# Subtracting the low parts of 64 weight tiles on VectorE between the passes of the expert selection, instead of on GpSimd

## The chip, the cores and the metric

The kernel runs on one core of a Trainium2 chip. The metric is the device time of one execution in microseconds (us); lower is better. The engines are named as the profile names them: PE (TensorE), DVE (VectorE), ACT (ScalarE), POOL (GpSimd) and SP (SyncE, which here only issues DMAs).

## The reference: what is computed

One decoder layer for 512 tokens of width 2048: an attention and state-space mixer, a normalisation, and then a layer of very many small experts (PEER). Only the expert layer matters here:

```
s1, s2 = q[..., :half] @ sub_keys1.T, q[..., half:] @ sub_keys2.T      # 128 scores per side and head
v1, i1 = top_k(s1, 16);  v2, i2 = top_k(s2, 16)
cand = v1[..., :, None] + v2[..., None, :]                              # 256 sums per head
top_s, pos = top_k(cand, 16);  ids = cand_id[pos];  g = softmax(top_s)  # 8 heads x 16 experts a token
act = gelu(einsum('td,tkd->tk', h, u_tab[ids]))
out = einsum('tk,tkd->td', g * act, v_tab[ids])
```

There are 16384 experts, each with a row of 2048 numbers in `u_tab` and one in `v_tab`. The kernel does not gather these rows for three of the four blocks of 128 tokens: it multiplies the 384 tokens of these blocks with all experts, and weighs the products with a matrix of gates that is zero where an expert was not picked.

## The kernel before, in words

The products are wanted in nearly full float32 precision. So each operand is cut into a high part (ACT rounds it to fp32r, a format that PE multiplies fast) and a low part (the value less its high part), and each product is three matmuls: high by high, high by low, low by high.

The expert weights come in units of 128 x 1024. For a unit of `u_tab`, SP loads it into one of four buffers (`pre_raw`), ACT writes the high part into one of two places of `split` (line 861), an engine subtracts it from the raw unit and writes the low part beside it, and PE runs 24 matmuls of 128 x 384 (line 1615). Because `split` has two places, ACT may write the high part of unit n only when PE is done with unit n-2, and the low part of n can only follow.

The stage of this case lies between 1277 and 1720 us. It is called the expert selection, and goes over the four blocks of tokens m = 0 to 3. In each block:

- DVE runs `select(m)` (lines 1210 to 1250). It finds the best 16 of 128 scores in 16 rows (8 heads by 2 sides) in four passes: the largest 8 (MAX8, line 1191), their places and their removal (FIND_INDEX8 and MATCH_REPLACE8, lines 1194 and 1195), the next 8 (line 1198), their places (line 1201). Then it forms the 256 sums (line 1221), runs the same four passes over 8 rows of 256, and turns the places into expert numbers (lines 1224 to 1240; the longest steps are lines 1235 to 1237, which run twice). From line 1242 on it needs the exponentials of line 879.
- Beside it PE runs `ahead(m)`: 16 units, that is 16 x 24 matmuls, whose results do not depend on the selection. There are 64 such units "made ahead" in all. In the kernel before, POOL subtracts the low parts (line 643).
- ACT writes the high parts, applies the GELU to finished pairs of units, and only after the last unit of the block computes the exponentials (line 879) that line 1242 on DVE waits for.
- Then PE turns the picks of block m (for m = 0 to 2), and makes the gates of block m-1 (line 1638), while DVE writes the one-hot matrices for them (`one_hots`, lines 1258 and 1261). Only then does PE go on to `ahead(m+1)`.

Each engine takes its instructions in the order in which they are written, and a semaphore wait at the head holds back all that stands behind it. After each dependent step of the selection DVE waits for its own last instruction (`step`). After a block, the gates are stored by SP, and from block 2 on SP issues the loads of the next block's units only behind these stores.

Of the kernel before, what the change touches and what calls it, by code (L numbers as in the profile page):

```python
# [19 lines left out]
TB = S // P  # L20
# [12 lines left out]
PH, PK = 8, 16  # L33
# [10 lines left out]
RAWS = 4  # L44
# [7 lines left out]
WIN_PAIRS = AHEAD * GT // TB // 2  # L52
WIN_UNITS = 4 * WIN_PAIRS

F32 = mybir.dt.float32
# [3 lines left out]
ALU = mybir.AluOpType  # L59
# [51 lines left out]
def over(ap, axis, n):  # L111

    wide = ap.unsqueeze(axis)
    shape = list(wide.shape)
    shape[axis] = n
    return wide.to_broadcast(shape)
# [95 lines left out]
def decoder_layer(nc, x_rows, x_cols, c_cols, pos_cols, w_ada, b_ada_cols, w_slices, conv_w, conv_b,  # L212
                  dt_bias, a_log, d_skip, norm_w, sinks, w_out, ln1_g, ln1_b, w_q, keys, u_units, u_tab, v_tab,
                  ln2_g, ln2_b, out):
    with ExitStack() as ctx:
        def sb(name, shape, dt=F32):
            return ctx.enter_context(nc.sbuf_tensor(name, shape, dt))
# [14 lines left out]
        def place(region, off, *dims):  # L232

            start = taken.get(region, off)
            taken[region] = start + math.prod(dims)
            return at(start, *dims)
# [52 lines left out]
        split = sb("split", [P, 2, 2, UNIT], F32R)  # L289
# [90 lines left out]
        pair_v = place("e", WIN + 4 * K, PH, PK)  # L380
        pair_i = place("e", WIN + 4 * K, PH, PK).bitcast(U32)
# [13 lines left out]
        pre_raw = wt  # L395
# [186 lines left out]
        def _(pool):  # L582
# [53 lines left out]
                        .then_inc(wout_split, 1)  # L636


            for m in range(TB):
                with pool.Fori(0, WIN_PAIRS) as i:  # L640
                    for j in range(4):
                        pool.wait_ge(pre_high, i * 4 + (m * WIN_UNITS + j + 1))
                        nc.gpsimd.tensor_tensor(split[:, j % 2, 1, :], pre_raw[:, j, :], split[:, j % 2, 0, :].bitcast(F32), ALU.subtract)\  # L643
                            .then_inc(pre_split, 1)

            pool.wait_ge(topk_done, TB)
            pool.wait_ge(g_ps, DT // 4 + HOTS * OH // 4)
# [271 lines left out]
        def _(dve):  # L919
# [154 lines left out]
            with dve.Fori(0, TB) as b:  # L1074
                step = Steps(dve, dve_own, b * MIX_STEPS + start)
# [100 lines left out]
            with dve.Fori(0, TB) as m:  # L1176
                step = Steps(dve, dve_own, m * 10 + start1, held)
# [7 lines left out]
                assert step.n == 10, step.n  # L1185
            own.n += TB * 10

            def best16(rows, step):

                for values, _, source, _ in rows:  # L1190
                    ins = nc.vector.max(values[:, 0:8], source)
                step(ins)
                for values, indices, source, scratch in rows:
                    nc.vector.max_index(indices[:, 0:8], values[:, 0:8], source)
                    ins = nc.vector.match_replace(scratch, values[:, 0:8], source, NEG)
                step(ins)
                for values, _, _, scratch in rows:
                    ins = nc.vector.max(values[:, 8:16], scratch)
                step(ins)
                for values, indices, _, scratch in rows:  # L1200
                    ins = nc.vector.max_index(indices[:, 8:16], values[:, 8:16], scratch)
                step(ins)


            dve.wait_ge(h2_high, 1)
# [7 lines left out]
            def select(m):  # L1213
                step = Steps(dve, dve_own, m * TOP_STEPS + start2, held)
                dve.wait_ge(sc_ready, m + 1)
                dve.sem_inc(held, 1)
                best16([(top_v[:, side, h, :], top_i[:, side, h, :], sc[:, side, h, :], rest[:, side, h, :])
                        for side in range(2) for h in range(PH)], step)
                step(nc.vector.tensor_copy(top_f, top_i))

                step(nc.vector.tensor_tensor(cand, over(top_v[:, 0, :, :], 3, PK), over(top_v[:, 1, :, :], 2, PK), ALU.add))
                flat = [cand[:, h, :, :].rearrange("p a b -> p (a b)") for h in range(PH)]
                best16([(pair_v[:, h, :], pair_i[:, h, :], flat[h], flat[h]) for h in range(PH)], step)
                step(nc.vector.tensor_copy(pick_sum, pair_v[:, :, 0]))
                nc.vector.tensor_tensor(pair_v, pair_v, over(pick_sum, 2, PK), ALU.subtract).then_inc(pair_sub, 1)

                nc.vector.tensor_scalar(part_u[:, 0, :, :], pair_i, 4, None, ALU.logical_shift_right)
                step(nc.vector.tensor_scalar(part_u[:, 1, :, :], pair_i, 15, None, ALU.bitwise_and))
                step(nc.vector.tensor_copy(part_f, part_u))
                dve.wait_ge(parts_read, m + 1)  # L1230
                dve.sem_inc(held, 1)
                for side in range(2):
                    flat = hits.rearrange("p a b c -> p (a b) c")
                    places = part_f[:, side, :, :].rearrange("p a b -> p (a b)")
                    step(nc.vector.tensor_tensor(flat, over(iota[:, 0:PK], 1, PICKS), over(places, 2, PK), ALU.is_equal))
                    step(nc.vector.tensor_tensor(hits, hits, over(top_f[:, side, :, :], 2, PK), ALU.mult))
                    step(nc.vector.tensor_reduce(part_id[:, side, :, :].rearrange("p a b -> p (a b)"), flat, AX, ALU.add))
                step(nc.vector.scalar_tensor_tensor(part_f[:, 0, :, :], part_id[:, 0, :, :], float(NKEY), part_id[:, 1, :, :],
                                                    ALU.mult, ALU.add))
                nc.vector.tensor_copy(ids[:, bass.ds(m, 1), :].rearrange("p a (b c) -> p (a b) c", c=PK), part_f[:, 0, :, :])  # L1240
                dve.wait_ge(pair_exp, m + 1)
                step(nc.vector.tensor_reduce(pick_sum, pair_v, AX, ALU.add))
                step(nc.vector.reciprocal(pick_sum, pick_sum))
                nc.vector.tensor_tensor(gates[:, bass.ds(m, 1), :].rearrange("p a (b c) -> p (a b) c", c=PK), pair_v,
                                        over(pick_sum, 2, PK), ALU.mult).then_inc(topk_done, 1)
                dve.wait_ge(topk_done, m + 1)
                dve.sem_inc(sc_used, 1)
                assert step.n == TOP_STEPS, step.n

            def one_hots(m):  # L1250
# [4 lines left out]
                for n in range(P // OH):  # L1255
# [7 lines left out]
                    ins.then_inc(hot_ready, 1)  # L1263

            select(0)
            for m in range(1, TB):
                select(m)
                one_hots(m - 1)
# [98 lines left out]
            with dve.Fori(0, TB) as m:  # L1367
                step = Steps(dve, dve_own, m * 8 + start3, held)
# [381 lines left out]
```

## Time and profile before

| | |
|---|---|
| median of 3 runs | 3778.11 us (3774.91 to 3784.14) |
| time of the profiled execution | 3775.31 us |
| its span | 3773.7 us |
| busy over the span | PE 84%, DVE 67%, POOL 33%, ACT 27% |
| mean granted TensorE clock | 0.927 of full speed |
| low parts on POOL (line 643) | 64 instructions, 178.6 us busy, median 2398 ns, longest 4318 ns |
| stage of the expert selection | first MAX8 at 1277.40 us, last exponentials wanted at 1719.82 us |

The span runs from the first to the last instruction; the time of the execution is 1.6 us longer. Busy shares are averages over very different stages: the main loop over the experts begins after 1800 us and does not contain the lines of this case. In a timeline row stand the start, the time taken, the engine, line and operation, what is written and read, the number of instructions merged into the row, and in brackets how long the engine sat idle before it and what ended this.

### The profile page before, as it was taken

What the parts mean: (1) busy time and instruction counts of PE and PEld (TensorE: products, weight loads), DVE (VectorE), ACT (ScalarE), POOL (GpSimd) and SP (SyncE); (2) the same over time, 40 slices, a digit from 0 to 9 for tenths busy, and PEclk for the clock granted to TensorE, in tenths of its full rate; (3) what the DMA queues carried; (4) which work ended last, traced back from release to release, by engine and by line L of the source; (5) the groups of instructions that cost most, each with busy time, mean ns of one, the idle gap of its engine ahead of it and who ended that gap; (6) DMA issues with size and microseconds to landing.
All of it is one profiled execution on the core that took longest, in us unless ns stands there. A gap on an engine that the chain in (4) does not pass through costs nothing.

```text
span 3773.7 us, 45789 instructions
## 1 busy us (share of the span) xinstructions
PE 3156.9 (84%) x15577; PEld 2749.2 (73%) x15577; DVE 2510.1 (67%) x3254; ACT 1032.4 (27%) x1423; POOL 1235.6 (33%) x831
## 2 busy tenths in 40 slices
PE   0788975667957996875799999999999999999990
PEld 0666765556843685875677999999999999999980
DVE  7485544442142477696676788777778877777876
ACT  0212232223121232332222333333333333333321
POOL 1466640002410251431011344334344433444424
PEclk9999986668978998998899999999999999999995
DMA  9476540003211433244676788888888888888881
GB/s 394 176 305 238 219 163 0 0 0 112 95 39 47 149 122 129 97 164 172 199 224 211 266 298 291 301 294 299 303 301 294 290 302 295 299 303 301 294 297 45
DMA packets 255802, 785.55 MB, mean 208 GB/s; under 512 B 117488, under 2 KB 125808, under 8 KB 205680
## 3 DMA queue, kind: packets, MB, share of 16 engines
q1 hardware_dynamic: 205040, 476.30, 37.0%
q0 software_dynamic: 46080, 302.01, 21.5%
q10 hardware_dynamic: 4608, 6.29, 0.5%
q8 instruction: 42, 0.69, 0.1%
q14 instruction: 32, 0.26, 0.0%
HBM read 744.68 MB, written 39.85 MB: 208 GB/s over the span
## 4 chain that ended last, share of the span: by engine, by line
PE 56%; issue 30%; POOL 8%; DVE 4%; DMA 1%; ACT 1%; POOLq 0%; DVEq 0%; ACTq 0%; SPq 0%
PE ps L1685 28%; PE ps L1615 22%; PE ps L1402 6%; POOL split L643 3%; POOL win_parts L614 3%; POOL wout_parts L635 2%; DVE arena L1261 1%; DVE arena L1371 1%; DVE arena L1370 1%; DMA below_parts<-acts_ahead 1%; DVE arena L1280 1%; DVE arena L1258 0%; ACT win_parts L701 0%; PE ps L1385 0%; DVE arena L1167 0%
## 5 line engine op out<-in xcount | busy, mean ns | idle before, releaser
L1615 PE MATMUL ps<-h_parts,split 128*128 128x384 f32 x6144 | 1084.8, 336 | 31.1 <-POOL split L643 30.7
L1685 PE MATMUL ps<-split,w_parts 128*128 128x512 f32 x4608 | 1061.2, 390 | 51.6 <-DVE split L1319 33.1
L1615 PEld LDWEIGHTS ps<-h_parts,split 128*128 128x128 f32 x6144 | 1071.2, 188 | 41.7 <-issue 32.5
L1685 PEld LDWEIGHTS ps<-split,w_parts 128*128 128x128 f32 x4608 | 864.6, 188 | 235.4 <-DVE split L1319 33.2
L897 ACT ACTIVATE split<-below_parts 128x1024 fp32r<-128x1024 f32 x448 | 475.7, 1062 | 1299.5 <-PE ps L1685 742.6
L1319 DVE TENSOR_TENSOR split<-below_parts,split 128x1024 fp32r<-128x1024 f32 x448 | 548.9, 1225 | 396.4 <-ACT split L897 392.6
L655 POOL COPY arena<-arena 128x1 uint32 x256 | 185.9, 726 | 1069.6 <-DVE arena L1304 544.1
L643 POOL TENSOR_TENSOR split<-below_parts,split 128x1024 fp32r<-128x1024 f32 x64 | 178.6, 2794 | 461.8 <-ACT split L861 461.8
L1304 DVE SCALAR_TENSOR_TENSOR arena<-arena 128x2048 f32<-128x2048 f32 x128 | 300.7, 2349 | 2.7 <-DVE arena L1296 2.2
L614 POOL TENSOR_TENSOR win_parts<-arena,win_parts 128x512 fp32r<-128x512 f32 x128 | 229.8, 1800 | 208.0 <-ACT win_parts L701 207.1
L1285 DVE CUSTOM_DVE_ANT_0 arena<-arena 128x2048 f32<-128x2048 f32 x128 | 292.5, 2285 | 0.0
L658 POOL DMA_INDIRECT arena<-in_v_tab,arena x128 | 238.0, 1860 | 110.7 <-POOL arena L655 102.6
L658 POOL DMA_INDIRECT arena<-in_u_tab,arena x128 | 235.8, 1842 | 103.6 <-POOL arena L655 103.6
L963 DVE SCALAR_TENSOR_TENSOR arena<-arena,c_act 128x2048 f32<-128x2048 f32 x90 | 258.3, 2870 | 9.4 <-DMA arena<-in_w_ada 3.0
L1280 DVE TENSOR_TENSOR arena<-arena,ps 128x1024 f32<-128x1024 f32 x192 | 230.7, 1216 | 25.8 <-PE ps L1685 25.8
L1402 PE MATMUL ps<-win_parts,h_parts 128*128 128x512 f32 (+1 forms) x960 | 217.0, 384 | 30.4 <-POOL win_parts L614 30.4
L635 POOL TENSOR_TENSOR wout_parts<-below_parts,wout_parts 128x1024 fp32r<-128x1024 f32 x32 | 76.8, 2403 | 459.1 <-ACT wout_parts L813 459.1
L1402 PEld LDWEIGHTS ps<-win_parts,h_parts 128*128 128x128 f32 x960 | 172.6, 195 | 74.2 <-POOL win_parts L614 43.7
L1425 PE MATMUL ps<-ident,arena 128*128 128x128 f32 x345 | 74.3, 391 | 164.6 <-DVE arena L1184 64.7
L1425 PEld LDWEIGHTS ps<-ident,arena 128*128 128x128 f32 x345 | 64.1, 212 | 171.1 <-DVE arena L1184 66.3
L1402 PE MATMUL ps<-h_parts,win_parts 128*128 128x512 f32 x576 | 144.4, 407 | 25.7 <-POOL win_parts L614 23.1
L701 ACT ACTIVATE win_parts<-arena 128x512 fp32r<-128x512 f32 x128 | 80.4, 631 | 306.9 <-PE ps L1402 225.1
(224 smaller groups left out, 2849.1 us busy)
## 6 DMA issues: line engine op xcount, KB each, us to landing
below_parts<-in_u_units SPq DMA_DIRECT2D x256, 512.0 KB, 4.6
below_parts<-in_v_tab SPq DMA_DIRECT2D x256, 512.0 KB, 6.4
arena<-in_w_ada SPq DMA_DIRECT2D x96, 1024.0 KB, 7.4
arena<-in_w_slices POOLq DMA_DIRECT2D x64, 512.0 KB, 4.6
gates_by_expert<-arena SPq DMA_DIRECT2D x24, 1024.0 KB, 3.9
below_parts<-gates_by_expert SPq DMA_DIRECT2D x32, 768.0 KB, 8.5
below_parts<-in_w_out SPq DMA_DIRECT2D x32, 512.0 KB, 3.5
below_parts<-in_w_q SPq DMA_DIRECT2D x16, 512.0 KB, 3.5
```

The costliest lines, as they stand in the source:

```text
L614: nc.gpsimd.tensor_tensor(win_parts[:, j, 1, :], win_raw[slot][:, j, :], win_parts[:, j, 0, :].bitcast(F32), ALU.subtract)\
L643: nc.gpsimd.tensor_tensor(split[:, j % 2, 1, :], pre_raw[:, j, :], split[:, j % 2, 0, :].bitcast(F32), ALU.subtract)\
L658: nc.gpsimd.indirect_dma_start(out=ring[slot], out_offset=None, in_=table[:, :], in_offset=bass.IndirectOffsetOnAxis(ap=idx[:, slot:slot + ...
L897: nc.scalar.activation(split[:, j % 2, 0, :], raw[:, j % RAWS, :], ACT.Copy).then_inc(high_done, 1)
L963: nc.vector.scalar_tensor_tensor(acc, ada[:, k % 4, :], c_act[:, k:k + 1], acc, ALU.mult, ALU.add)\
L1280: nc.vector.tensor_tensor(row, row, wide(2 * m, UNIT), ALU.add).then_inc(v_read, 1)
L1285: nc.vector.tensor_tensor_reduce(out=ring[slot], in0=ring[slot], in1=h2_now, scale=1.0, scalar=0.0, op0=ALU.mult, op1=ALU.add, accum_out=a ...
L1304: nc.vector.scalar_tensor_tensor(acc_v, ring[slot], w4[:, q:q + 1], acc_v, ALU.mult, ALU.add).then_inc(row_used, 1)
L1319: nc.vector.tensor_tensor(split[:, j % 2, 1, :], raw[:, j % RAWS, :], split[:, j % 2, 0, :].bitcast(F32), ALU.subtract)\
L1402: ins = nc.tensor.matmul(ps[:, m, 0:cols], lhs, rhs, start=k == 0 and n == 0, stop=k == KT - 1 and n == 2)
L1615: ins = nc.tensor.matmul(ps[:, 6 + b, 0:DT], lhs[:, cols], h2_parts[:, rhs, k, :], start=k == 0 and n == 0, stop=k == KT - 1 and n == 2)
L1685: ins = nc.tensor.matmul(ps[:, 2 * m + b, :], w_parts[:, buf, lhs, i, m * P:(m + 1) * P], rhs[:, b * 512:(b + 1) * 512], start=i == 0 and ...
```

## The change

POOL's loop over the low parts goes. DVE gets a helper `pre_low(m, n)` that waits for the high part of unit n of block m and subtracts it, and it calls this helper 16 times inside `select(m)`: in the passes over 16 rows after the eighth row and at the end (units 0 to 5), after the cast and after the sums (6, 7), after each of the last three passes over 8 rows (8, 9, 10), before the one-hot comparison (11), and two at a time after each of the two reductions of line 1237 (12, 13 and 14, 15).

```
-            for m in range(TB):
-                with pool.Fori(0, WIN_PAIRS) as i:
-                    for j in range(4):
-                        pool.wait_ge(pre_high, i * 4 + (m * WIN_UNITS + j + 1))
-                        nc.gpsimd.tensor_tensor(split[:, j % 2, 1, :], pre_raw[:, j, :], split[:, j % 2, 0, :].bitcast(F32), ALU.subtract)\
-                            .then_inc(pre_split, 1)
...
+            def pre_low(m, n):
+
+                dve.wait_ge(pre_high, m * WIN_UNITS + n + 1)
+                nc.vector.tensor_tensor(split[:, n % 2, 1, :], pre_raw[:, n % RAWS, :], split[:, n % 2, 0, :].bitcast(F32), ALU.subtract)\
+                    .then_inc(pre_split, 1)
+
+            def best16(rows, step, m, n):
+
+                def low_after(r):
+
+                    if r % 8 == 7:
+                        pre_low(m, n + r // 8)
+
+                for r, (values, _, source, _) in enumerate(rows):
                     ins = nc.vector.max(values[:, 0:8], source)
                 step(ins)
+                for r, (values, indices, source, scratch) in enumerate(rows):
                     nc.vector.max_index(indices[:, 0:8], values[:, 0:8], source)
                     ins = nc.vector.match_replace(scratch, values[:, 0:8], source, NEG)
+                    if r < len(rows) - 1:
+                        low_after(r)
                 step(ins)
+                low_after(len(rows) - 1)
+                n += len(rows) // 8
...
                 step(nc.vector.tensor_copy(top_f, top_i))
+                pre_low(m, 6)
...
                 step(nc.vector.tensor_tensor(cand, over(top_v[:, 0, :, :], 3, PK), over(top_v[:, 1, :, :], 2, PK), ALU.add))
+                pre_low(m, 7)
...
                 step(nc.vector.tensor_copy(part_f, part_u))
+                pre_low(m, 11)
...
                     step(nc.vector.tensor_reduce(part_id[:, side, :, :].rearrange("p a b -> p (a b)"), flat, AX, ALU.add))
+                    pre_low(m, 12 + 2 * side)
+                    pre_low(m, 13 + 2 * side)
```

On DVE, at the head of the selection of block 0, the kernel before runs the second pass of line 1194 and 1195 without a break:

```order
L1194 MAX_INDEX arena<-arena 128x8
L1195 MATCH_REPLACE arena<-arena 128x128
L1194 MAX_INDEX arena<-arena 128x8
L1195 MATCH_REPLACE arena<-arena 128x128
L1194 MAX_INDEX arena<-arena 128x8
```

In the changed kernel (where these are lines 1199 and 1200) the first low part, line 1185, stands behind the eighth row, after MAX8 over all 16 rows and half of the second pass:

```order
L1199 MAX_INDEX arena<-arena 128x8
L1200 MATCH_REPLACE arena<-arena 128x128
L1185 TENSOR_TENSOR split<-below_parts,split 128x1024
L1199 MAX_INDEX arena<-arena 128x8
L1200 MATCH_REPLACE arena<-arena 128x128
```

So nothing of unit 0's low part is made before DVE has come that far. At the other end of the same `select(0)` on DVE, the kernel before has the long steps of the expert numbers back to back:

```order
L1235 TENSOR_TENSOR arena<-iota,arena 128x2048
L1236 TENSOR_TENSOR arena<-arena 128x2048
L1237 TENSOR_REDUCE arena<-arena 128x128
L1235 TENSOR_TENSOR arena<-iota,arena 128x2048
L1236 TENSOR_TENSOR arena<-arena 128x2048
L1237 TENSOR_REDUCE arena<-arena 128x128
L1238 SCALAR_TENSOR_TENSOR arena<-arena 128x128
L1240 CAST arena<-arena 128x128
L1242 TENSOR_REDUCE arena<-arena 128x8
```

And in the changed kernel, where line 1254 is the former 1235 and line 1263 the former 1242:

```order
L1185 TENSOR_TENSOR split<-below_parts,split 128x1024
L1254 TENSOR_TENSOR arena<-iota,arena 128x2048
L1255 TENSOR_TENSOR arena<-arena 128x2048
L1256 TENSOR_REDUCE arena<-arena 128x128
L1185 TENSOR_TENSOR split<-below_parts,split 128x1024 x2
L1254 TENSOR_TENSOR arena<-iota,arena 128x2048
L1255 TENSOR_TENSOR arena<-arena 128x2048
L1256 TENSOR_REDUCE arena<-arena 128x128
L1185 TENSOR_TENSOR split<-below_parts,split 128x1024 x2
L1259 SCALAR_TENSOR_TENSOR arena<-arena 128x128
L1261 CAST arena<-arena 128x128
```

The low parts of the last two units stand behind nearly the whole selection. On POOL the 64 instructions of line 643 are gone, and what stood behind them (the gathers) stands directly behind the loop of line 635, with the same waits as before.

## Rows read from the trace of the kernel before

**Rows 1.** Part 5 of the page (costliest groups): one DVE subtraction of this shape.
```profile
L1319 DVE TENSOR_TENSOR split<-below_parts,split 128x1024 fp32r<-128x1024 f32 x448 | 548.9, 1225 | 396.4 <-ACT split L897 392.6
```

**Rows 2.** Waits, 1250 to 1850 us: waiter, releaser, total, times, longest.
```profile
DVE arena L1242 <- ACT arena L879: 82.7, 4, 27.0
...
PE ps L1615 <- POOL split L643: 30.7, 14, 11.1
```

**Rows 3.** Timeline of DVE, block 0.
```profile
1277.40 3.19 DVE L1191 MAX8 arena<-arena 128x8 f32<-128x128 f32 x16 [104.75 <-ACT arena L834]
...
1289.33 3.20 DVE L1198 MAX8 arena<-arena 128x8 f32<-128x128 f32 x16
...
1299.97 2.79 DVE L1191 MAX8 arena<-arena 128x8 f32<-128x256 f32 x8
...
1316.25 2.42 DVE L1227 TENSOR_SCALAR arena<-arena 128x128 uint32<-128x128 uint32 x1
1318.59 0.21 DVE L1228 TENSOR_SCALAR arena<-arena 128x128 uint32<-128x128 uint32 x1
...
1319.51 2.29 DVE L1235 TENSOR_TENSOR arena<-iota,arena 128x2048 f32<-128x2048 f32 x1 [0.26 <-DVE arena L1229]
1321.95 4.25 DVE L1236 TENSOR_TENSOR arena<-arena 128x2048 f32<-128x2048 f32 x1
...
1331.21 4.24 DVE L1236 TENSOR_TENSOR arena<-arena 128x2048 f32<-128x2048 f32 x1
...
1338.04 0.29 DVE L1238 SCALAR_TENSOR_TENSOR arena<-arena 128x128 f32<-128x128 f32 x1 [0.15 <-DVE arena L1237]
...
1353.10 0.29 DVE L1242 TENSOR_REDUCE arena<-arena 128x8 f32<-128x128 f32 x1 [14.40 <-ACT arena L879]
```

**Rows 4.** Timeline of POOL, block 0: the low parts of units 7, 9, 10, 12.
```profile
1307.74 2.40 POOL L643 TENSOR_TENSOR split<-below_parts,split 128x1024 fp32r<-128x1024 f32 x1 [2.33 <-ACT split L861]
...
1316.06 2.52 POOL L643 TENSOR_TENSOR split<-below_parts,split 128x1024 fp32r<-128x1024 f32 x1 [1.77 <-ACT split L861]
1320.22 3.81 POOL L643 TENSOR_TENSOR split<-below_parts,split 128x1024 fp32r<-128x1024 f32 x1 [1.64 <-ACT split L861]
...
1329.79 3.52 POOL L643 TENSOR_TENSOR split<-below_parts,split 128x1024 fp32r<-128x1024 f32 x1 [1.33 <-ACT split L861]
```

**Rows 5.** Timeline of PE: units 5 to 9 of block 0.
```profile
1302.13 21.08 PE L1615 MATMUL ps<-h_parts,split 128*128 128x384 f32 x120 [0.30 <-POOL split L643]
```

**Rows 6.** Timeline of DVE: start of block 1, line 1242 of the others.
```profile
1356.34 3.19 DVE L1191 MAX8 arena<-arena 128x8 f32<-128x128 f32 x16 [2.17 <-ACT arena L834]
...
1433.01 0.29 DVE L1242 TENSOR_REDUCE arena<-arena 128x8 f32<-128x128 f32 x1 [14.40 <-ACT arena L879]
...
1579.27 0.28 DVE L1242 TENSOR_REDUCE arena<-arena 128x8 f32<-128x128 f32 x1 [26.97 <-ACT arena L879]
...
1719.82 0.28 DVE L1242 TENSOR_REDUCE arena<-arena 128x8 f32<-128x128 f32 x1 [26.97 <-ACT arena L879]
1720.25 0.20 DVE L1243 RECIPROCAL arena<-arena 128x8 f32<-128x8 f32 x1
...
1721.18 1.23 DVE L1258 TENSOR_TENSOR arena<-iota,arena 128x1024 f32<-128x1024 f32 x1 [0.29 <-DVE arena L1244]
1722.32 2.13 DVE L1261 TENSOR_SCALAR arena<-iota,arena 128x128 f32<-128x128 f32 x8
```

**Rows 7.** Timeline of blocks 2 and 3: first high parts, first units of block 2.
```profile
1500.88 1.06 ACT L861 ACTIVATE split<-below_parts 128x1024 fp32r<-128x1024 f32 x1 [6.89 <-DMA below_parts<-in_u_units]
...
1504.49 10.48 PE L1615 MATMUL ps<-h_parts,split 128*128 128x384 f32 x48 [11.14 <-POOL split L643]
...
1640.79 1.06 ACT L861 ACTIVATE split<-below_parts 128x1024 fp32r<-128x1024 f32 x1 [6.27 <-DMA below_parts<-in_u_units]
```

**Rows 8.** Stretches of 2 us at block 2: length, PE, PEld, DVE, ACT, POOL busy, clock, DMA.
```profile
1494.00:1496.00 2.00, 0.00 (x0) 0.00 (x0) 1.85 (x15) 0.00 (x0) 0.00 (x0) 1.00 0.63 262
...
1498.00:1500.00 2.00, 0.00 (x0) 0.00 (x0) 2.00 (x17) 0.00 (x0) 0.00 (x0) 0.58 0.94 375
...
1506.00:1508.00 2.00, 2.00 (x8) 2.00 (x7) 1.85 (x16) 0.00 (x0) 0.68 (x1) 0.50 0.77 250
...
1508.00:1510.00 2.00, 2.00 (x12) 2.00 (x11) 2.00 (x17) 0.00 (x0) 0.00 (x0) 0.86 0.66 240
```

More of the change, by code:

```diff
@@ L1186, in _ @@
             own.n += TB * 10
-            def best16(rows, step):
-                for values, _, source, _ in rows:
+            def pre_low(m, n):
[7 more added lines that the diff above has]
+                for r, (values, _, source, _) in enumerate(rows):
                     ins = nc.vector.max(values[:, 0:8], source)
                 step(ins)
-                for values, indices, source, scratch in rows:
+                for r, (values, indices, source, scratch) in enumerate(rows):
                     nc.vector.max_index(indices[:, 0:8], values[:, 0:8], source)
                     ins = nc.vector.match_replace(scratch, values[:, 0:8], source, NEG)
+                    if r < len(rows) - 1:
+                        low_after(r)
                 step(ins)
-                for values, _, _, scratch in rows:
+                low_after(len(rows) - 1)
+                n += len(rows) // 8
+                for r, (values, _, _, scratch) in enumerate(rows):
                     ins = nc.vector.max(values[:, 8:16], scratch)
+                    if r < len(rows) - 1:
+                        low_after(r)
                 step(ins)
-                for values, indices, _, scratch in rows:
+                low_after(len(rows) - 1)
+                n += len(rows) // 8
+                for r, (values, indices, _, scratch) in enumerate(rows):
                     ins = nc.vector.max_index(indices[:, 8:16], values[:, 8:16], scratch)
+                    if r < len(rows) - 1:
+                        low_after(r)
                 step(ins)
+                low_after(len(rows) - 1)
             dve.wait_ge(h2_high, 1)
@@ L1217, in select @@
                 best16([(top_v[:, side, h, :], top_i[:, side, h, :], sc[:, side, h, :], rest[:, side, h, :])
-                        for side in range(2) for h in range(PH)], step)
+                        for side in range(2) for h in range(PH)], step, m, 0)
                 step(nc.vector.tensor_copy(top_f, top_i))
+                pre_low(m, 6)
                 step(nc.vector.tensor_tensor(cand, over(top_v[:, 0, :, :], 3, PK), over(top_v[:, 1, :, :], 2, PK), ALU.add))
+                pre_low(m, 7)
                 flat = [cand[:, h, :, :].rearrange("p a b -> p (a b)") for h in range(PH)]
-                best16([(pair_v[:, h, :], pair_i[:, h, :], flat[h], flat[h]) for h in range(PH)], step)
+                best16([(pair_v[:, h, :], pair_i[:, h, :], flat[h], flat[h]) for h in range(PH)], step, m, 8)
                 step(nc.vector.tensor_copy(pick_sum, pair_v[:, :, 0]))
```

## The prediction

> **What bounds the kernel now.** The page comes first: PE is busy for 84% of the span and DVE for 67%, but that is an average, and the change touches only the selection stage. So I went on to the waits of that stage, where two rows matter [rows 2]. DVE's line 1242 waits 82.7 us in 4 waits for ACT's exponentials, which stand behind the last of a block's 16 units; and PE waits 30.7 us in 14 waits for POOL's low parts. Then the timelines. In block 0 DVE is through with all that it can do at 1338.7 and sits idle for 14.40 us until 1353.10 [rows 3]; in block 1 the wait is the same, and in blocks 2 and 3 it is 26.97 us [rows 6]. The end of a block is thus set by PE's 16 units: units 5 to 9 run as one row [rows 5], and POOL's low parts, released once per unit, start 8.32 us apart for units 7 and 9 and 4.16 us apart for 9 and 10 [rows 4]. So a unit costs PE 4.16 us. Block 0's low part of unit 12 ends at 1329.79 + 3.52 = 1333.31; units 12 to 15 then take 16.64 and end at about 1350.05 (0.1 us for the start), and line 1242 starts at 1353.10. The tail from PE's last unit to line 1242 is 3.05 us. After line 1242 the block's remainder, the gates, the stores and the next block follow in a chain, so what line 1242 loses in a block, the kernel loses.
>
> **The change, term by term.** DVE gets 64 subtractions. One lasts 1.225 us [rows 1]; how long it holds DVE is the distance to the next start behind a 128x1024 subtraction-like instruction, 1722.32 - 1721.18 = 1.14 [rows 6]. I take 1.16, so 16 x 1.16 = 18.6 us a block. By amount, that nearly fits into idle times of 14.4 and 27.0. But DVE takes instructions in written order, so what matters is when each low part comes.
>
> *First low part.* In block 0 MAX8 begins at 1277.40, line 1198 at 1289.33, 11.93 later; the second pass lies between 3.34 and 11.93, and unit 0's low part stands in its middle, 7.6 us after the start [rows 3]. PE starts 1.22 + 0.06 later, at 8.9.
>
> *Units 0 to 7.* Here DVE has only 22.6 us of work up to unit 7's place (1299.97 - 1277.40) [rows 3], plus 7 x 1.16 = 8.1, and PE is slower, so DVE stalls on high parts. Unit 7's low part needs the high part that ACT writes after PE's unit 5. In block 0 PE started unit 5 at 1302.13, so it ended at 1306.29, and low part 7 began at 1307.74: 1.45 us behind [rows 4, 5]. Until unit 0 PE has at most some scores to compute and then idles, so I let the first two units run as in block 2, 10.48 us for 48 matmuls after an idle time of 11.14 [rows 7]. Unit 5 ends at 8.9 + 0.3 + 10.5 + 4 x 4.16 = 36.3, and low part 7 starts at 37.8. DVE has stalled 7.1 us by then.
>
> *Units 8 to 15.* Now DVE is the slower one. Between unit 7's place and unit 14's (1338.04, line 1238) lie 38.07 us of work before [rows 3], and seven low parts add 8.1. Against this stands a gain. Line 1227 takes 2.42 us for 128 elements, its twin line 1228 only 0.21, and 1228 starts at 1318.59, when POOL's low part (1316.06 + 2.52) ends. Line 1236 takes 4.25 us where line 1235, of the same size, takes 2.29. POOL's low part 10 starts inside line 1235, lasts 3.81 instead of 2.4, and ends at 1324.03; line 1236 ends 2.17 later, at 1326.20. For the second one the end of POOL's low part 12, 1333.31, and DVE's, 1335.45, are 2.14 apart [rows 3, 4]. So each holds the other up for whole instructions, and without POOL's DVE saves 2.2 + 2 x 1.96 = 6.1 us a block. Low part 14 starts at 37.8 + 38.1 - 6.1 + 8.1 = 77.9.
>
> The Trainium skill, "SBUF — State Buffer", section Who interferes with whom, says that a VectorE instruction with two SBUF inputs and a GpSimd one that reads SBUF exclude each other for a whole instruction. The opposite reading is also at hand: line 1236 takes 4.25 and 4.24 us, as if that were its own speed. By the rule the trace's constancy is a lock step, and the sum is as above; by the other reading 4 x 6.1 us more is lost (a rival below). The ends 2.14 and 2.17 us after POOL's speak for the rule.
>
> *End.* PE's units 14 and 15 come behind low part 14: 77.9 + 1.28 + 8.32 = 87.5, and with the tail 90.5 us from DVE's start to line 1242. This is the core of the forecast: two whole units and the tail stand behind nearly all of DVE's selection and 14 low parts.
>
> | block | line 1242 before | after, alone | loss |
> |---|---|---|---|
> | 0 | 1353.10 | 1277.40 + 90.5 = 1367.9 | 14.8 |
> | 1 | 1433.01 | 1356.34 + 90.5 = 1446.8 | 13.8 |
> | 2 | 1579.27 | 1502.0 - 7.6 + 90.5 = 1584.9 | 5.6 |
> | 3 | 1719.82 | 1641.9 - 7.6 + 90.5 = 1724.8 | 5.0 |
>
> In blocks 2 and 3 unit 0's high part is the last to come, since its load stands behind the gates' stores: 1500.88 + 1.06 + 0.1 = 1502.0, and 1640.79 + 1.06 + 0.1 = 1641.9 [rows 7]. There DVE used to have a head start, which it now waits away at unit 0. Sum 39.2 us.
>
> *Clock.* In block 2 the granted clock was 1.00 at 1494 to 1496 with PE idle, 0.58 at 1498 to 1500, 0.50 at 1506 to 1508 with PE busy again, 0.86 after that [rows 8]: it went from 2.4 to 1.2 GHz a few microseconds into the idle time. The new gap before unit 8 is 5 us by this walk (low part 8 comes 9.5 + 1.2 behind low part 7, while PE has only units 6 and 7's rest). If the clock falls there, two units lose 2.1 us, of which DVE's wait for the high part of unit 10 passes 1.9 on: 7.8 us over four blocks. Bounds 0 and 7.8; I take the middle, 3.9, since 5 us is near what it took to fall.
>
> *At no cost:* the loads into `pre_raw`, which wait for low parts 4 units back (a lead of 4 x 4.16 = 16.6 us for one load; were it too short, ACT would wait for a load, as it does at the head of blocks 2 and 3); and POOL, whose gathers wait for the end of the stage anyway.
>
> Total 43 us. The profiled execution took 3775.31 (span 3773.7 and 1.6 around it), so 3818; the median of the runs is 2.8 above it, so 3821. I say 3820.
>
> **Bounds.** A low part could hold DVE for 1.10 to 1.40 us (the duration plus a semaphore's price); only seven of them lie on the path, so -2 to +7 us over four blocks. Lock gain: 0 to 6.1 us a block, taken 6.1. Slow first units: 1.1 us a block less if the clock holds. From these: 3775.31 + 2.8 + 34 - 2 = 3810 to 3778 + 39 + 7.8 + 7 + 24 = 3856, all at once.
>
> **Rivals.**
> *A, the idle time covers it; the kernel gets faster.* DVE's 82.7 us of idle time exceed 64 x 1.16 = 74 us, and a low part takes half as long as on POOL. If the places kept pace with PE's 4.16 us, PE would lose its waits on POOL but the two that the loads set (11.1 and nearly as much): 30.7 - 21.7 = 9.0 us, giving 3769. It decides where low part 14 starts earlier than 63.0 us after DVE's start in block 0 (75.7 before, less 1.28 + 8.32 + 3.05 behind it). Against it: DVE's own work up to that place is 60.6 - 6.1 = 54.5 us, and with 14 low parts 70.7, even if DVE never stalls. If it holds only in blocks 2 and 3, where 27 us are idle, the kernel stays within 0.3%.
> *B, no relief from the lock.* Lines 1227 and 1236 are slow of themselves: 43 + 24 = 67 us, 3845. For it: the constant duration. Against it: the ends tied to POOL's.
> *C, the clock falls at every gap* (before units 8, 12 and 14): about 2.8 us a block more than the walk without clock, 39 + 11 = 50 us, 3828.
> *D, DVE does not stall early* because the first units run at full clock: 39 - 4 = 35 us, 3813.
>
> **How the numbers follow.** Forecast with C and D, which differ in size only, 0.80; B 0.10; A 0.05 for faster, and 0.05 for its partial form within 0.3%. About 0.3% (11 us) is what a measurement of this kernel tells from no change. So slower 0.90, same 0.05, faster 0.05. The range leaves out A and most of B: 3800 (the 35 of D, with DVE stalling some 3 us a block less than walked) to 3841.
>
> **What would show it right or wrong.** DVE's line 1255 (1236 before) falls from 4.25 to 2.29 us, and 1245 (1227) to about 0.2; PE waits at units 0, 8, 12 and 14 for line 1185, at 8 for about 5 us; the first MAX8 of a block to line 1263 takes 90 us in blocks 0 and 1 instead of 75.7 and 76.7; the wait of 1263 for the exponentials shrinks to about 9 us (87.5 + 3.0 less DVE's end at some 81). Nothing behind the stage changes its length. Wrong if PE's units follow each other without gaps over 1 us, or if the main loop after 1800 us changes.

## The result, and the profile after

The changed kernel takes 3824.51 us (median of 4 runs, 3821.89 to 3829.41), against 3776.51 us for the kernel before in the same comparison: a ratio of 1.0126, 95% interval 1.0106 to 1.0145. It is 48 us slower. Timed a second time beside other kernels it gave 1.0131 (1.0116 to 1.0146).

The profiled execution has a span of 3825.2 us, 51.5 more than before. Its stage of the selection runs from the first MAX8 at 1284.80 to line 1263 of block 3 at 1772.11, so 487.3 us against 442.4 [rows 3, 6]: 44.9 us. What lies behind it has kept its length (2053.1 against 2053.9 us). What lies ahead of it is 7.4 us longer, though none of that code was changed; over all profiles of this study the first MAX8 stands between 1272 and 1285 us, so I take that for scatter between executions and read everything below from stretches inside the stage.

Who waits for whom in the stage (waiter, releaser, total, times, longest), in the changed kernel, to be held against [rows 2]:

```profile
PE ps L1636 <- DVE split L1185: 59.9, 12, 9.2
DVE split L1185 <- ACT split L855: 51.4, 38, 2.7
...
DVE arena L1263 <- ACT arena L873: 31.9, 4, 8.0
```

The idle time of DVE at the end of the blocks has shrunk from 82.7 to 31.9 us, as the new work would make one expect. But 51.4 us have come up inside the selection, where DVE stands at a low part and waits for ACT's high part, and PE now waits 59.9 us for low parts, in 12 waits: three in each block. The timeline of PE in block 0 shows which three (start, time taken, number of matmuls, idle time before):

```profile
1293.67 35.30 PE L1636 MATMUL ps<-h_parts,split 128*128 128x384 f32 x192 [6.91 <-DVE split L1185]
1333.68 19.07 PE L1636 MATMUL ps<-h_parts,split 128*128 128x384 f32 x96 [4.71 <-DVE split L1185]
1355.36 18.48 PE L1636 MATMUL ps<-h_parts,split 128*128 128x384 f32 x96 [2.61 <-DVE split L1185]
```

192 matmuls are eight units: PE stands before units 0, 8 and 12. On DVE, in the same block (rows between left out; the low parts shown are those of units 0, 7, 10, 11, 14 and 15):

```profile
1284.80 3.19 DVE L1196 MAX8 arena<-arena 128x8 f32<-128x128 f32 x16 [104.67 <-ACT arena L828]
1292.33 1.21 DVE L1185 TENSOR_TENSOR split<-below_parts,split 128x1024 fp32r<-128x1024 f32 x1
...
1321.78 1.23 DVE L1185 TENSOR_TENSOR split<-below_parts,split 128x1024 fp32r<-128x1024 f32 x1 [0.73 <-ACT split L855]
1322.92 2.71 DVE L1196 MAX8 arena<-arena 128x8 f32<-128x256 f32 x8
...
1341.40 1.23 DVE L1185 TENSOR_TENSOR split<-below_parts,split 128x1024 fp32r<-128x1024 f32 x1 [0.69 <-ACT split L855]
...
1343.07 0.22 DVE L1245 TENSOR_SCALAR arena<-arena 128x128 uint32<-128x128 uint32 x1
...
1345.56 1.23 DVE L1185 TENSOR_TENSOR split<-below_parts,split 128x1024 fp32r<-128x1024 f32 x1 [1.70 <-ACT split L855]
1346.70 2.29 DVE L1254 TENSOR_TENSOR arena<-iota,arena 128x2048 f32<-128x2048 f32 x1
1349.13 2.29 DVE L1255 TENSOR_TENSOR arena<-arena 128x2048 f32<-128x2048 f32 x1
...
1363.59 1.22 DVE L1185 TENSOR_TENSOR split<-below_parts,split 128x1024 fp32r<-128x1024 f32 x1
1366.65 1.22 DVE L1185 TENSOR_TENSOR split<-below_parts,split 128x1024 fp32r<-128x1024 f32 x1 [1.84 <-ACT split L855]
...
1376.42 0.29 DVE L1263 TENSOR_REDUCE arena<-arena 128x8 f32<-128x128 f32 x1 [7.97 <-ACT arena L873]
```

Two things are to be seen. A low part holds DVE for 1322.92 - 1321.78 = 1.14 us. And lines 1245 and 1255, which are 1227 and 1236 of before, take 0.22 and 2.29 us instead of 2.42 and 4.25 [rows 3]. Grouped over the whole stage, changed kernel (the last two numbers are busy us and mean ns, then idle time):

```profile
L1255 DVE TENSOR_TENSOR arena<-arena 128x2048 f32<-128x2048 f32 x8 | 18.3, 2292 | 1.2
...
L1245 DVE TENSOR_SCALAR arena<-arena 128x128 uint32<-128x128 uint32 x4 | 0.9, 223 | 0.0
```

The clock, in stretches of 2 us: one in the middle of units 0 to 7, then those around the idle times before units 8 and 12 (length, PE, PEld, DVE, ACT, POOL busy, granted clock, DMA share, GB/s):

```profile
1308.00:1310.00 2.00, 2.00 (x13) 2.00 (x13) 1.22 (x5) 1.06 (x1) 0.00 (x0) 1.00 0.81 298
...
1328.00:1330.00 2.00, 0.97 (x6) 0.65 (x4) 2.00 (x11) 0.99 (x2) 0.00 (x0) 1.00 0.00 0
1330.00:1332.00 2.00, 0.00 (x0) 0.00 (x0) 2.00 (x11) 0.45 (x2) 0.00 (x0) 0.90 0.26 94
1332.00:1334.00 2.00, 0.32 (x1) 0.33 (x2) 1.85 (x4) 0.00 (x0) 0.00 (x0) 0.50 0.01 4
1334.00:1336.00 2.00, 2.00 (x7) 2.00 (x7) 2.00 (x7) 0.00 (x0) 0.00 (x0) 0.50 0.59 182
...
1338.00:1340.00 2.00, 2.00 (x12) 2.00 (x12) 2.00 (x11) 0.00 (x0) 0.00 (x0) 0.90 0.59 184
...
1354.00:1356.00 2.00, 0.64 (x2) 0.65 (x3) 1.99 (x2) 0.22 (x1) 0.00 (x0) 0.87 0.27 98
1356.00:1358.00 2.00, 2.00 (x8) 2.00 (x7) 2.00 (x2) 0.00 (x0) 0.00 (x0) 0.50 0.79 231
```

Before unit 8 it fell from 2.4 to 1.2 GHz (1.00 to 0.50) within the idle time, and PE then had 7 matmuls in a stretch of 2 us instead of the 13 at the full clock. At unit 12, after 2.61 us of idle time, it fell again (0.87, then 0.50), but here only when PE was already at work. PE resumed at 1355.36, and in stretches of half a microsecond the clock stands at 0.98 up to 1355.5 and at 0.50 from there on:

```profile
1355.00:1355.50 0.50, 0.14 (x1) 0.14 (x2) 0.50 (x2) 0.00 (x0) 0.00 (x0) 0.98 0.47 172
1355.50:1356.00 0.50, 0.50 (x2) 0.50 (x3) 0.50 (x1) 0.00 (x0) 0.00 (x0) 0.50 0.61 221
```

Block by block, from the end of one block (line 1242 before, 1263 after) to that of the next, and from the first MAX8 for block 0:

| block | before | after | loss | forecast |
|---|---|---|---|---|
| 0 | 75.70 | 91.62 | 15.9 | 14.8 |
| 1 | 79.91 | 95.35 | 15.4 | 13.8 |
| 2 | 146.26 | 153.31 | 7.1 | 5.6 |
| 3 | 140.55 | 147.03 | 6.5 | 5.0 |
| sum | | | 44.9 | 39.2, and 3.9 for the clock |

### The profile page after: what moved, and what is told of

Read it like the earlier page. It is cut to its first block, busy times and chain, and to the rows that moved or that the text cites. A ratio compares the mean times of both kernels' runs of the same rounds, so it can differ in the third digit from the quotient of the medians.

```text
span 3825.2 us, 45689 instructions
## 1 busy us (share of the span) xinstructions
PE 3180.2 (83%) x15577; PEld 2777.5 (73%) x15577; DVE 2558.1 (67%) x3318; ACT 1032.5 (27%) x1423; POOL 1050.5 (27%) x767
## 4 chain that ended last, share of the span: by engine, by line
PE 68%; issue 15%; DVE 11%; POOL 3%; ACT 2%; DMA 1%; POOLq 0%; DVEq 0%; ACTq 0%; SPq 0%
PE ps L1706 28%; PE ps L1636 27%; PE ps L1423 6%; PE ps L1581 4%; PE ps L1601 3%; DVE arena L1282 3%; POOL win_parts L614 3%; DVE arena L1279 1%; DVE arena L1392 1%; DVE arena L1391 1%; DMA below_parts<-acts_ahead 1%; DVE split L1185 1%; DVE arena L1301 1%; DVE arena L1199 0%; DVE arena L1161 0%
## 5 line engine op out<-in xcount | busy, mean ns | idle before, releaser
L1636 PE MATMUL ps<-h_parts,split 128*128 128x384 f32 x6144 | 1101.3, 339 | 59.9 <-DVE split L1185 59.9
L1636 PEld LDWEIGHTS ps<-h_parts,split 128*128 128x128 f32 x6144 | 1091.1, 192 | 66.9 <-issue 63.2
L1706 PE MATMUL ps<-split,w_parts 128*128 128x512 f32 x4608 | 1061.3, 390 | 50.5 <-DVE split L1340 31.9
L1423 PEld LDWEIGHTS ps<-win_parts,h_parts 128*128 128x128 f32 x960 | 178.9, 203 | 73.7 <-POOL win_parts L614 42.1
L1423 PEld LDWEIGHTS ps<-h_parts,win_parts 128*128 128x128 f32 x576 | 112.4, 198 | 59.7 <-POOL win_parts L614 33.2
```

What stands on the lines that cost most here:

```text
L1423: ins = nc.tensor.matmul(ps[:, m, 0:cols], lhs, rhs, start=k == 0 and n == 0, stop=k == KT - 1 and n == 2)
L1636: ins = nc.tensor.matmul(ps[:, 6 + b, 0:DT], lhs[:, cols], h2_parts[:, rhs, k, :], start=k == 0 and n == 0, stop=k == KT - 1 and n == 2)
L1706: ins = nc.tensor.matmul(ps[:, 2 * m + b, :], w_parts[:, buf, lhs, i, m * P:(m + 1) * P], rhs[:, b * 512:(b + 1) * 512], start=i == 0 and ...
```

## The experiments

In all of them the time is given as a ratio to the kernel before on the same chip. The stage is from the first MAX8 to the last line 1242 (or its successor) of the profiled execution; before it is 442.4 us.

| run | ratio, interval | stage, us |
|---|---|---|
| changed kernel | 1.0126 (1.0106 to 1.0145) | 487.3 |
| changed kernel again | 1.0131 (1.0116 to 1.0146) | 488.5 |
| even places | 0.9965 (0.9953 to 0.9978) | 430.5 |
| places only | 1.0043 (1.0028 to 1.0058) | 459.3 |
| work only | 1.0001 (0.9992 to 1.001) | 444.0 |
| last low parts up | 1.0066 (1.005 to 1.0083) | 469.3 |
| first low parts up | 1.0153 (1.0138 to 1.0168) | 499.2 |
| idle time of PE filled | 1.0098 (1.0083 to 1.0113) | 476.2 |
| even places, shared with POOL | 0.9965 (0.9953 to 0.9977) | 427.6 |

**Even places.** The same 64 subtractions, each called where a table says. The keys name a pass ("A1" to "A4" for the passes over 16 rows, "B1" to "B4" over 8), and the row ahead of which the call stands:

```
+            PLACES = [{('A1', 4): (0, 1), ('A2', 4): (2,), ('A2', 10): (3,), ('A2', 15): (4,), ('A3', 12): (5,), ('A4', 8): (6,), 'cand': (7,),
+                       ('B1', 2): (8,), ('B2', 1): (9,), ('B2', 5): (10,), ('B3', 1): (11,), ('B4', 1): (12,), 'picksum': (13,),
+                       ('mul', 0): (14,), ('red', 0): (15,)}, ...]
+            def low(key):
+                for n in PLACES[now[0]].get(key, ()):
+                    pre_low(now[0], n)
...
                 for r, (values, indices, source, scratch) in enumerate(rows):
+                    low((tag + "2", r))
                     nc.vector.max_index(indices[:, 0:8], values[:, 0:8], source)
```

> The changed kernel with the same 64 low parts on DVE, but at other places: each stands where DVE comes by about when PE needs it (units 0 and 1 behind the first few MAX8, the others about every 4.2 us of DVE's time, 15 before the second reduction at the latest; block 1 a little later, blocks 2 and 3 by some 10 us later, because their loads come late). Theory 'places': the 48 us come from where the low parts stand, not from how many there are. A block 0 then ends (line of the exponentials, counted from the first MAX8) at about 74 us, against 75.7 before and 91.6 in the changed kernel: 54.8 us of DVE's own work and 16 x 1.16 us. Stage 442.4 - 12 = about 430 us, kernel about 3765 (0.3% faster than before). Rival 'work': 74 us of new DVE work in a stage where DVE had 83 us idle cannot be hidden, wherever it stands: 3810 to 3825. In between (3780 to 3800) if stalls at places that miss by a microsecond add up.

Measured: 3764.05 us, 0.35% faster than the kernel before, where the theory said 3765; stage 430.5, where it said 430. PE's units of block 0 are a single row, and in blocks 0 and 1 the end of the block no longer waits for the exponentials (in blocks 2 and 3 it still waits 5.5 us). Timeline of PE, then of DVE, even places, block 0:

```profile
1282.19 66.83 PE L1635 MATMUL ps<-h_parts,split 128*128 128x384 f32 x384 [0.23 <-DVE split L1188]
```
```profile
1279.99 0.88 DVE L1200 MAX8 arena<-arena 128x8 f32<-128x128 f32 x4 [104.76 <-ACT arena L828]
1280.83 2.36 DVE L1188 TENSOR_TENSOR split<-below_parts,split 128x1024 fp32r<-128x1024 f32 x2
...
1353.69 0.28 DVE L1262 TENSOR_REDUCE arena<-arena 128x8 f32<-128x128 f32 x1
```

1353.69 - 1279.99 = 73.7 us, forecast 74. The work on DVE is that of the changed kernel; only its places differ. So the loss of 48 us comes from where the work stands, and the rival that 74 us of new work cannot be hidden anywhere falls.

**Places only.** POOL subtracts as before, and DVE, instead of subtracting, sets a mark (a copy of one element) at each place of the changed kernel:

```
-                dve.wait_ge(pre_high, m * WIN_UNITS + n + 1)
-                nc.vector.tensor_tensor(split[:, n % 2, 1, :], ...).then_inc(pre_split, 1)
+                nc.vector.tensor_copy(c_tmp[:, n:n + 1], ones[:, 0:1]).then_inc(marker, 1)
...
+                        pool.wait_ge(marker, i * 4 + (m * WIN_UNITS + j + 1))
                         pool.wait_ge(pre_high, i * 4 + (m * WIN_UNITS + j + 1))
```

> Low parts on POOL as before, but each waits also for a mark that DVE sets (a copy of one element) at the place where the changed kernel subtracts. So DVE has hardly any new work, and only the places act. Theory 'places and work together': PE starts its 16 units about 7.6 + 2.4 us after DVE, blocks 0 and 1 lose 5 to 6 us each, blocks 2 and 3 nothing (the loads come later than the first mark), because without the 18.6 us of low parts DVE is at every later place before PE needs it: about +11 us, 3789. If the places alone were the cause: +35 us or more.

Measured: stage +16.9 us, more than the 11 expected: 9.4 in block 0, 8.1 in block 1, nearly nothing in 2 and 3. PE in block 0:

```profile
1288.02 14.40 PE L1643 MATMUL ps<-h_parts,split 128*128 128x384 f32 x72 [6.74 <-POOL split L646]
1303.32 21.09 PE L1643 MATMUL ps<-h_parts,split 128*128 128x384 f32 x120 [0.90 <-POOL split L646]
```

It starts 10.2 us after the first MAX8 (1277.80), as expected, and then three units take 14.40 instead of some 12.8 us (8.6 for two units at the full clock in the rows below, and 4.16 more). The granted clock was 0.50 from 1286 to 1290: the low clock after the idle time, which this expectation had left out. Later places cost nothing.

**Work only.** POOL subtracts as before; DVE runs a reduction of 128x1024 at each place, without a wait. Its result is read by nobody:

```
-                nc.vector.tensor_tensor(split[:, n % 2, 1, :], ...).then_inc(pre_split, 1)
+                nc.vector.tensor_reduce(c_tmp[:, n:n + 1], tmp2[:, 0:1024], AX, ALU.add)
```

> Low parts on POOL as before, and at the 64 places DVE runs a reduction of 128x1024 (some 1.2 us, one input) whose result nobody reads, with no wait. Only DVE's work grows. Theory 'places and work together': DVE comes to the end of a block after 61.3 + 18.6 = 80 us, so blocks 0 and 1 lose 3 to 4 us each and blocks 2 and 3 nothing (27 us idle): about +8 us, 3786. If the amount of work alone were the cause: +40 us or more. Neither this run nor the one before reaches 48, nor their sum.

Measured: no difference, where 8 us more were expected. Block 0 lasts 80.3 us and block 1 loses 3.1, about as expected, but blocks 2 and 3 gain 1.9 and 4.3 us, which the expectation did not see. The waits say why (work only, same stage):

```profile
PE ps L1641 <- POOL split L644: 23.3, 4, 10.3
...
DVE arena L1268 <- ACT arena L880: 3.9, 1, 3.9
```

PE waits for POOL 4 times instead of 14 [rows 2]. The reductions have shifted DVE's long subtractions and multiplications against POOL's, and where they meet it is now DVE that comes second: lines 1259 and 1260 (1235 and 1236 before) take 3479 and 3764 ns in the mean, while POOL's low parts in block 3 take 2.4 to 2.9 us and PE's units of block 3 are one row of 384. So 77 us of additional work on DVE, in the idle time that the kernel before had, cost nothing net.

Places alone give 16.9 and work alone 1.6 us of the 44.9. The other 26.4 us appear only with both together. My reading is that each low part in the row delays the places of all that follow, and each wait for a high part does too; no run isolates this. The three numbers do not add up cleanly either: in both runs POOL still subtracts, so neither has the relief from POOL that the changed kernel has (line 1236's successor takes 4243 ns in the mean in places only, 3764 in work only, and 2292 in the changed kernel).

**Last low parts up.** As in the changed kernel, but units 12 to 15 stand before the lines ("mul", 0), ("red", 0), ("eq", 1) and ("mul", 1):

```
+                    low(("eq", side))
...
+                    low(("mul", side))
                     step(nc.vector.tensor_tensor(hits, hits, over(top_f[:, side, :, :], 2, PK), ALU.mult))
+                    low(("red", side))
                     step(nc.vector.tensor_reduce(part_id[:, side, :, :]...))
...
-                    pre_low(m, 12 + 2 * side)
-                    pre_low(m, 13 + 2 * side)
```

> The changed kernel with only the last four low parts of a block moved up: 12 before the multiplication of side 0, 13 before its reduction, 14 before the comparison of side 1, 15 before its multiplication (before: 12 and 13 behind the reduction of side 0, 14 and 15 behind that of side 1). Theory 'late last units': two to four whole units stand behind DVE's end, so a block ends 3 to 6 us earlier: stage 487 - 12 to 24, kernel 3800 to 3812. If the late start of unit 0 were what counts, nothing changes (3824).

Measured: stage 469.3, 18 us less than the changed kernel; ratio 1.0066 instead of 1.0126. PE in block 0 now stands only twice (last low parts up):

```profile
1286.34 35.31 PE L1635 MATMUL ps<-h_parts,split 128*128 128x384 f32 x192 [6.90 <-DVE split L1188]
1326.36 35.74 PE L1635 MATMUL ps<-h_parts,split 128*128 128x384 f32 x192 [4.70 <-DVE split L1188]
```

Four of sixteen places carry 40% of the loss.

**First low parts up.** Only units 0 and 1 stand earlier, behind the fourth and fifth MAX8; all others stand where they stand in the changed kernel:

```
-                    if r % 8 == 7:
-                        pre_low(m, n + r // 8)
...
+            PLACES = [{('A1', 4): (0,), ('A1', 5): (1,), ('A3', 8): (2,), ('A4', 0): (3,), ('A4', 8): (4,), 'topf': (5,), 'cand': (6,), ('B1', 0): (7,), ('B3', 0): (8,), ('B4', 0): (9,), 'picksum': (10,), ('eq', 0): (11,), ('eq', 1): (12, 13), 'stt': (14, 15)}, ...]
```

> The changed kernel with only units 0 and 1 moved up, to behind the fourth MAX8 of a block. PE then starts about 3 us after DVE in block 0 instead of 8.9. Theory 'the last places decide': what PE gains at the head it loses as idle time before unit 8, because DVE's own way to units 8 to 15 is hardly shorter; blocks 0 and 1 gain some 2 us each, and blocks 2 and 3 lose some 4 us each, since there DVE now stands still at its first row until the loads have come (about 9 us) instead of working through half of the second pass first. Sum between -2 and +6 against the changed kernel, 3822 to 3831. Rival 'the late first unit costs': 5 to 6 us a block would come back in blocks 0 and 1: 3812 or less.

Measured: slower still, 1.0153, stage 499.2. PE starts 3.4 us after DVE and then stands before unit 2:

```profile
1282.28 8.64 PE L1635 MATMUL ps<-h_parts,split 128*128 128x384 f32 x48
1295.99 26.82 PE L1635 MATMUL ps<-h_parts,split 128*128 128x384 f32 x144 [5.08 <-DVE split L1188]
1327.52 19.70 PE L1635 MATMUL ps<-h_parts,split 128*128 128x384 f32 x96 [4.71 <-DVE split L1188]
```

Blocks 0 and 1 gain nothing (I had expected 2 us each), and blocks 2 and 3 lose 4.8 and 6.3 us, since DVE stands behind its fourth MAX8 until the loads have come. So moving the first units alone brings nothing while the later places stand where they do. It is not free for all that: with the later places kept up (places only), the late start cost 9.4 and 8.1 us in blocks 0 and 1. The sum was outside what I had written (-2 to +6; measured +12 in the stage, +8 in the time against the changed kernel of the same comparison).

**Idle time of PE filled.** The changed kernel, with matmuls that nobody reads put before PE's waits for units 8 and 12:

```
+                        for _ in range({(2, 0): 26, (3, 0): 12}.get((n, j), 0)):
+                            nc.tensor.matmul(ps[:, 4, 0:DT], h2_parts[:, 0, 0, 0:P], h2_parts[:, 0, 0, :], start=True, stop=True)
                         pe.wait_ge(pre_split, n * 4 + (m * WIN_UNITS + j + 1 + RAWS))
```

> The changed kernel; PE also runs 26 matmuls of 128x384 that nobody reads just before its wait for the low part of unit 8, and 12 before that of unit 12, in time in which it is idle anyway (4.7 and 2.6 us). If the granted clock falls in those gaps and this costs time, units 8 to 11 take 17.0 instead of 19.07 us, and a block 1.6 to 2.1 us less: stage 487 - 6 to 8, kernel 3817. If the lower clock is hidden by DVE's own lateness, or the fill gets in the way: 3824 to 3828.

The run differs from the changed kernel in two more things: PE's loop over n is written out, and PE waits for one more semaphore (`g_staged`) ahead of the first fill. Neither was run by itself.

Measured: stage 476.2, 11 us less than the changed kernel with no useful work added or taken away; 3811.88 against 3825.39 us for the changed kernel of the same comparison. Timeline of PE, block 0, fill on line 1627, and the clock in the two idle times that are now filled:

```profile
1316.65 4.67 PE L1627 MATMUL ps<-h_parts 128*128 128x384 f32 x26
1321.44 17.12 PE L1640 MATMUL ps<-h_parts,split 128*128 128x384 f32 x96
1338.41 2.25 PE L1627 MATMUL ps<-h_parts 128*128 128x384 f32 x12
1341.02 8.62 PE L1640 MATMUL ps<-h_parts,split 128*128 128x384 f32 x48 [0.37 <-DVE split L1185]
1350.61 8.61 PE L1640 MATMUL ps<-h_parts,split 128*128 128x384 f32 x48 [0.97 <-DVE split L1185]
```
```profile
1318.00:1320.00 2.00, 2.00 (x14) 2.00 (x13) 2.00 (x11) 0.29 (x1) 0.00 (x0) 1.00 0.27 98
...
1340.00:1342.00 2.00, 1.63 (x9) 1.31 (x8) 2.00 (x2) 0.04 (x1) 0.00 (x0) 1.00 0.27 98
```

The granted clock stays at 1.00. Units 8 to 11 take 17.12 instead of 19.07 us, 8.6 us less over the four blocks (17.12 to 17.15 us against 19.07 to 19.51). Units 12 to 15 gain 0.3 us a block, because with the clock held up PE also stands before unit 14 (0.97 us), which it did not in the changed kernel. That is 9.7 of the 11.1 us, at the places that the fill can reach; the other 1.4 are spread over the rest of the blocks and were not traced. In all the low clock cost some 2.8 us a block.

**Even places, shared with POOL.** In blocks 0 and 1 POOL subtracts for units 2 to 5, which fall into passes with one input, and DVE's other twelve stand at new places; blocks 2 and 3 are those of even places:

```
+            for m in range(2):
+                for n in range(2, 6):
+                    pool.wait_ge(pre_split, m * WIN_UNITS + n + RAWS)
+                    pool.wait_ge(pre_high, m * WIN_UNITS + n + 1)
+                    nc.gpsimd.tensor_tensor(split[:, n % 2, 1, :], ..., ALU.subtract).then_inc(pre_split, 1)
```

> Even places as in the first run; in blocks 0 and 1 POOL subtracts the low parts of units 2 to 5, which fall into passes of MAX8 and FIND_INDEX8 (one input, no lock), and DVE the other twelve, at places set anew. DVE has 4.6 us less to do in these blocks, so PE and not DVE sets their end: 71.8 us instead of 73.7 in block 0, some 74.3 instead of 75.5 in block 1. Stage 430.5 - 3 to 4, kernel 3760 to 3762. Rival: the hand-over between the two engines costs a microsecond or two at unit 2 or 6, and nothing is left of the gain: 3764 to 3767.

Measured: 3762.68 us, ratio 0.9965, the same as even places without POOL. The stage is 427.6 us, 2.8 less. Block 0 has the forecast step (71.6 us against 73.7; forecast 71.8), but block 1 is 0.8 us longer, where the hand-over to POOL costs PE one wait of 1.20 us, and 1.5 of the 2.8 us come from blocks 2 and 3, where the two versions do not differ. So only block 0 bears out the idea, and its gain is too small for the times to tell. Both versions beat both given kernels.

**The changed kernel again.**

> The changed kernel once more, beside the others on one chip. Its profile had the first MAX8 at 1284.8 us, 7.4 us later than the kernel before, though nothing ahead of it differs on DVE or PE. If that belongs to the change, it comes again; if it was that execution, the first MAX8 is at 1277 to 1280, the stage again at 487 us and the time about 3822.

Measured: 3825.39 us; first MAX8 at 1281.67, stage 488.5. The stage repeats to 1.2 us. The start of the stage lies in between and settles nothing beyond the scatter; the difference between the 48 us timed and the 45 to 46 of the stage is within the interval.

## Why the prediction was right

Forecast 3820 us, measured 3824.5; forecast +43, measured +48 (44.9 in the stage).

- *The idle time does not cover it, because DVE takes its instructions in order.* Shown by even places (same work, 57 us less in the stage) and by work only (77 us of work, 1.6 us in the stage net; POOL's share in this is told above).
- *Low part 0 comes 7.6 us after the start*: 7.53.
- *DVE stalls on high parts up to unit 7, which starts at 37.8*: 36.98.
- *Unit 8 is late by about 5 us*: 4.71, in every block.
- *Lock relief of 6.1 us a block*: lines 1245 and 1255 fell to 0.22 and 2.29 us, all 4 and all 8 of them. Rival B falls. The constant 4.25 us of line 1236 was a lock step with POOL: 4246 ns in the mean with POOL beside it and 2292 without, and all 8 ended 2.14 to 2.17 us after a low part of POOL's. The Trainium skill ("SBUF — State Buffer", Who interferes with whom) says that a VectorE instruction with two inputs in SBUF contends with a GpSimd one that reads SBUF. This trace agrees. Line 1227 has only one such input; that it waited as well is shown by its own 2.42 us, which shrank to 0.22.
- *Low part 14 starts at 77.9*: 78.79.
- *The end of the block hangs on low part 14*: not as put. 91.6 and 92.1 us came out for 90.5, but PE ran units 12 to 15 without a break (96 matmuls in 18.48 us), so low part 14 was not what it waited for. The last wait was for low part 12, and then the first of these units ran for some 3 us at the low clock. Without that (idle time filled) PE does wait at unit 14. The tail of 3.05 us was mis-read too. It rests on units 12 to 15 of the kernel before ending at 1350.05, but their row ends at 1333.43 + 17.09 = 1350.52, and the tail is 2.58 us, as it is in the changed kernel (1376.42 less 1373.84). That made the walk 0.5 us a block too long.

```profile
1333.43 17.09 PE L1615 MATMUL ps<-h_parts,split 128*128 128x384 f32 x96 [0.49 <-POOL split L643]
```

- *Clock*: mis-sized. I took 3.9 us, half of 7.8, for a fall before unit 8 alone. The clock fell there in every block, and units 8 to 11 paid 8.6 us for it, so the full 7.8 was the better size and the halving was the error. It fell at unit 12 as well, and filling both idle times gives back 11 us. The walk without this term was in turn too long: 39.2 us against 476.2 - 442.4 = 33.8 in the filled run. Of these 5.4 us the mis-read tail explains 1.9; the rest was not traced. Two errors of 5 and 7 us nearly cancelled in the sum, so its closeness is partly luck. Rival C (clock falls at every gap, +50) describes the mechanism better than my main line, though the gap before unit 14 that it counts did not come up; its time, 3828, is as near as mine.
- *Rival A (faster)* failed at these places, and is true at others: with even places PE never stands inside a block, and the kernel gains 13 us, more than the 9 that A had for it, since the units also start earlier (in block 0 2.2 us after the first MAX8 instead of 3.4).

## What to carry to other kernels

Work moved onto an engine with enough idle time is only free if each piece stands where the engine comes by when the piece is ready and before it is wanted; idle time at the end of a chain does not help a piece in its middle. When a short producer is woven by hand into another chain, lay out both timelines first, including what the chain loses to the pieces themselves, and place by due time, not by the structure of the loops. And an operation whose duration is constant can still be waiting: compare its end with the end of the neighbour on the other engine before calling the duration its own.

## What the runs showed of the hardware that was not expected

- DVE's two-input instructions and POOL's held each other up for whole instructions, in either direction. In the kernel before it was mostly both: POOL's subtraction grew from 2.40 to as much as 4.32 us and DVE's multiplication from 2.29 to 4.25. With DVE's timing shifted (work only) all but two of POOL's 64 low parts kept 2.4 to 2.9 us and DVE paid instead (3.5 and 3.8 us on average). PE, which depends on POOL, then waited for it inside a block only twice, 1.25 and 1.39 us, where the two others (4.18 and 4.24 us) stood. In the meetings looked at, the one that came second was lengthened: in the kernel before DVE's line 1235 began at 1328.77 and POOL's low part at 1329.79 took 3.52 us; in work only POOL began at 1333.26 and DVE's comparison at 1333.63 took 4.18.
- 38 useless matmuls a block, put into 7.3 us in which PE was idle, made the stage 11 us shorter, and the granted clock stayed at 2.4 GHz where it had fallen to 1.2.
